# Gate maps of 32 of 48 quads of tokens built between the last 16 tiles of expert_u

## What is computed

```
act = gelu(einsum('td,tkd->tk', xt, expert_u[it]))
out = einsum('tk,tkd->td', gt * act, expert_v[it])
```

## Time and profile before

| | us |
|---|---|
| median of 3 runs | 1657.08 (1656.9 to 1657.41) |
| span of the profiled execution | 1656.2 |
| expert_u, tile 48 to the end of tile 62 (15 tiles) | 86.97 |
| gate stage, last tile of expert_u to the last map | 74.24 |
| expert_v, steady part | 286.44 |
| PE busy over the span | 1553.5 (94%) |
| DVE, ACT, POOL busy | 930.0, 688.0, 558.9 |

### The profile page before, as it was taken

One profiled execution on the slowest core, in us unless ns is written; L12 is line 12 of the kernel. 1 busy time (PEld: TensorE's weight loads), 2 busy tenths in 40 slices (PEclk: granted clock), 3 DMA queues, 4 the chain that ended last, 5 costly groups with the idle time before them and its releaser, 6 DMA issues.

```text
span 1656.2 us, 23309 instructions
## 1 busy us (share of the span) xinstructions
PE 1553.5 (94%) x9505; PEld 1219.7 (74%) x9505; DVE 930.0 (56%) x1472; ACT 688.0 (42%) x1017; POOL 558.9 (34%) x323
## 2 busy tenths in 40 slices
PE   7999999998898888999999999999998789999998
PEld 6788744443343434988899999999998668888886
DVE  5876422111111113686453887798434988988886
ACT  6565411101001003574453453444445975555554
POOL 3201100000000001322122434344555978787771
PEclk9999999999999999999999999999999999999999
DMA  8435999999999998535344555555566029999994
GB/s 295 145 120 194 422 399 421 421 421 421 421 421 421 421 421 342 197 128 191 102 157 152 190 192 187 173 201 184 197 232 215 1 96 337 348 347 349 357 340 161
DMA packets 99342, 444.80 MB, mean 269 GB/s; under 512 B 11152, under 2 KB 19856, under 8 KB 57632
## 3 DMA queue, kind: packets, MB, share of 16 engines
q1 hardware_dynamic: 86256, 404.90, 65.2%
q0 software_dynamic: 11264, 33.60, 5.5%
q10 hardware_dynamic: 1712, 4.76, 0.7%
HBM read 435.26 MB, written 7.86 MB: 268 GB/s over the span
## 4 chain that ended last, share of the span: by engine, by line
PE 66%; DMA 19%; DVE 7%; ACT 5%; issue 2%; POOL 0%; ACTq 0%; SPq 0%; DVEq 0%
DMA big<-in_w_up 11%; PE ps L483 11%; PE ps L485 11%; PE ps L484 11%; PE ps L1184 11%; PE ps L680 8%; PE ps L1176 7%; DMA fix<-in_w_up 3%; DMA hh<-in_w_up 3%; DVE fix_parts L1221 1%; PE ps L1152 1%; DMA fix<-in_w_in 1%; ACT fix_parts L2104 1%; ACT y L2522 1%; PE ps L663 1%
## 5 line engine op out<-in xcount | busy, mean ns | idle before, releaser
L2567 POOL TENSOR_TENSOR fix_parts<-fix,fix_parts 128x512 fp32r<-128x512 f32 x59 | 143.5, 2434 | 698.6 <-ACT fix_parts L2104 698.5
L485 PE MATMUL ps<-hh_parts,fix_parts 128*128 128x256 f32 x1120 | 317.3, 283 | 0.0
L680 PE MATMUL ps<-big 128*64 128x512 f32 x800 | 249.2, 595 | 17.8 <-DMA big<-in_w_up 9.2
L1221 DVE TENSOR_TENSOR fix_parts<-fix,fix_parts 128x1536 fp32r<-128x1536 f32 (+1 forms) x84 | 171.0, 2036 | 115.9 <-ACT fix_parts L2104 113.7
L483 PE MATMUL ps<-hh_parts,fix_parts 128*128 128x256 f32 x768 | 219.2, 285 | 6.8 <-issue 5.9
L484 PE MATMUL ps<-hl_parts,fix_parts 128*128 128x256 f32 x768 | 217.8, 284 | 0.0
L485 PEld LDWEIGHTS ps<-hh_parts,fix_parts 128*128 128x128 f32 x1120 | 215.2, 192 | 0.0
L680 PE MATMUL ps<-fix,big 128*64 128x512 f32 x528 | 189.4, 594 | 17.5 <-DMA big<-in_w_up 9.0
L2104 ACT ACTIVATE fix_parts<-fix 128x2048 fp32r<-128x2048 f32 x84 | 160.8, 1915 | 69.8 <-PE ps L1184 56.4
L680 PEld LDWEIGHTS ps<-big 128*64 128x64 f32 x800 | 79.7, 137 | 110.8 <-issue 110.0
L483 PEld LDWEIGHTS ps<-hh_parts,fix_parts 128*128 128x128 f32 x768 | 147.7, 192 | 8.2 <-issue 8.1
(11 more groups left out here) (416 smaller groups left out, 3664.4 us busy)
## 6 DMA issues: line engine op xcount, KB each, us to landing
fix<-in_expert_u SPq DMA_DIRECT2D x64, 1024.0 KB, 5.3
fix<-in_expert_v SPq DMA_DIRECT2D x38, 1024.0 KB, 7.6
big<-in_w_up SPq DMA_DIRECT2D x34, 1024.0 KB, 26.6
big<-in_w_down SPq DMA_DIRECT2D x34, 1024.0 KB, 25.6
big<-in_w_gate SPq DMA_DIRECT2D x32, 1024.0 KB, 26.1
big<-in_expert_v SPq DMA_DIRECT2D x26, 1024.0 KB, 7.5
fix<-in_w_gate SPq DMA_DIRECT2D x23, 1024.0 KB, 26.4
fix<-in_w_up SPq DMA_DIRECT2D x22, 1024.0 KB, 26.7
```

Source lines behind the costliest of these rows:

```text
L485: return pe.matmul(o, l[1], r[0], start=False, stop=last)
L680: ins = pe.matmul(m.PS[64 * i:64 * i + 64, bank, :], lhs(h * k_of // 2 + k, i), view(t.place[t.slot[x]])[:, k, c0:c0 + 512], start=(h + k ...
L1221: nc.vector.tensor_tensor(m.fr(x[:, 0:end]), x[:, 0:end], m.fr(hi[:, 0:end]).bitcast(F32), ALU.subtract).then_inc(s.lo_v, 1)
L2567: nc.gpsimd.tensor_tensor(m.fr(x[:, at:2048]), x[:, at:2048], m.fr(hi[:, at:2048]).bitcast(F32), ALU.subtract).then_inc(s.lo_g, 1)
```

## The change

`EARLY_AT = 48` and `EARLY = 32`. Behind the matmuls of each of the tiles 48 to 63 of expert_u, PE makes the maps of two quads, 32 in all (`early_quads`); the quads 32 to 47 follow after the last tile, as before.

- The one-hots of the early quads lie in three new places (two in `DS`, one in `Y`); the first wait for no tile. Each engine writes those of quads 2(i - 48) and 2(i - 48) + 1 in its iteration i: ACT after the high part of tile i + 1 and ahead of the gelus of tile i; DVE ahead of the low part of tile i + 1; POOL likewise.
- DVE weighs the two quads of iteration i - 1 in iteration i, in two instructions each: rows of `W` whose gelu is there are multiplied, the rows to come get a copy of the map.
- A tile from 48 on has its gelu of the tokens already mapped (8 to 128 of them) laid into `EA`, and DVE multiplies it into the maps in `W` (`weigh_acts`); ACT has three activations then, over the same 512 columns.
- DVE's `NG` (the negated gates) moves to the end of iteration 47. In the remaining quads DVE weighs two quads behind, not one.
- POOL fetches one sparse row at tile 48, since the places of the other two now hold one-hots; those two are fetched between the fourth and fifth pick, after the one-hots. The row sums begin in iteration 4 of expert_v instead of 3 (`sum_at`).

```diff
-    return 3 + a * 60 // SPARSE
+    return 4 + a * 59 // SPARSE
+def early_quads(i):
+    return range(2 * (i - EARLY_AT), 2 * (i - EARLY_AT) + 2) if EARLY_AT <= i < 64 else range(0)
+def early_from(q):
+    return EARLY_AT + q // 2
+def early_tokens(i):
+    return 8 * max(i - EARLY_AT + 1, 0)
...
+    rings = [DS[:, 2048:3072], DS[:, 3072:4096], part(512, 1024)], [EB[i // 2][:, 1024 * (i % 2):1024 * (i % 2) + 1024] for i in range(4)]
+    slot = lambda q: rings[0][q % 3] if q < EARLY else rings[1][q % 4]
+    m.EA = [DS[:, 256 * i:256 * i + 256] for i in range(2)]
...
+    def gate_map(q):
+        bank = q % 4
+        for sem in (s.e_a, s.e_v, s.e_g):
+            pe.wait_ge(sem, q + 1)
+        if q >= 4:
+            pe.wait_ge(s.weighed, q - 3)
+        for x in range(4):
+            ins = pe.matmul(m.PS[:, bank, x * P:(x + 1) * P], m.E1[q][:, x * P:(x + 1) * P],
+                            m.E2[q][:, x * P:(x + 1) * P], start=True, stop=True)
+        ins.then_inc(s.ghot, 1)
...
+        for q in early_quads(i):
+            gate_map(q)
+    for q in range(EARLY, DENSE // 4):
+        gate_map(q)
...
+def slot_open(eng, s, t, q):
+    if q < EARLY:
+        if q >= 3:
+            eng.wait_ge(s.ghot, q - 2)
+    elif q < EARLY + 4:
+        eng.wait_ge(s.used, t.used[t.first["expert_v"] - 1])
+    else:
+        eng.wait_ge(s.ghot, q - 3)
...
+    def weigh(q):
+        w, gates = m.W[:, :, 4 * q:4 * q + 4], m.PS[:, q % 4, :].rearrange("p (t n) -> p n t", t=4)
+        ve.wait_ge(s.ghot, q + 1)
+        if q >= EARLY:
+            ve.wait_ge(s.act, 64)
+            ve.tensor_tensor(w, gates, w, ALU.mult).then_inc(s.weighed, 1)
+            return
+        n = 2 * early_from(q)
+        ve.wait_ge(s.act, n // 2)
+        ve.tensor_tensor(w[:, 0:n, :], gates[:, 0:n, :], w[:, 0:n, :], ALU.mult)
+        ve.tensor_copy(w[:, n:P, :], gates[:, n:P, :]).then_inc(s.weighed, 1)
+    def weigh_acts(i):
+        tokens = early_tokens(i)
+        w = m.W[:, 2 * i:2 * i + 2, 0:tokens]
+        ve.wait_ge(s.act, i + 1)
+        ve.wait_ge(s.weighed, tokens // 4)
+        ve.tensor_tensor(w, m.EA[i % 2][:, 0:2 * tokens].rearrange("p (n t) -> p n t", n=2), w, ALU.mult).then_inc(s.early, 1)
+    for i in range(64):
+        for q in early_quads(i):
+            one_hots(q)
+        for q in early_quads(i - 1):
+            weigh(q)
+        dve_low(nc, m, s, t, first + i + 1)
+        if i > EARLY_AT:
+            weigh_acts(i - 1)
...
+    for q in range(EARLY, DENSE // 4):
+        one_hots(q)
+        weigh(q - 2)
+        if q - 2 == EARLY - 1:
+            weigh_acts(63)
...
+        tokens = early_tokens(i)
+        if tokens:
+            if i >= EARLY_AT + 2:
+                ac.wait_ge(s.early, i - EARLY_AT - 1)
+            ac.activation(m.EA[i % 2][:, 0:2 * tokens].rearrange("p (n t) -> p n t", n=2), src[:, :, SPARSE:SPARSE + tokens],
+                          ACT.Gelu_apprx_tanh)
+        ac.activation(m.W[:, 2 * i:2 * i + 2, tokens:DENSE], src[:, :, SPARSE + tokens:256], ACT.Gelu_apprx_tanh).then_inc(s.act, 1)
...
+    fetch(0)
+    for i in range(EARLY_AT, 64):
+        for q in early_quads(i):
+            one_hots(q)
+        if i < 63:
+            pool_low(nc, m, s, t, first + i + 1)
+    for q in range(EARLY, DENSE // 4):
+        one_hots(q)
...
+    po.wait_ge(s.ghot, EARLY)
+    for k in range(4):
+        pick(k)
+    for k in range(1, RING):
+        fetch(k)
+    for k in range(4, 8):
         pick(k)
```

More of the change, by code:

```diff
@@ L25 @@
 RING = 3
+EARLY_AT = 48
+EARLY = 32
 MOE_PLACES = (0, 1, 2, 3, 4, 5, 6, 9, 10, 11, 12, 13, 14, 15)
@@ L157, in signals @@
     s.ng, s.e_a, s.e_v, s.e_g = one("neg_gates"), one("one_hots_act"), one("one_hots_dve"), one("one_hots_pool")
-    s.ghot, s.weighed = one("gate_maps"), one("weighed")
+    s.ghot, s.weighed, s.early = one("gate_maps"), one("weighed"), one("acts_weighed")
     s.lists, s.moved, s.acts_kept = one("sparse_lists"), one("sparse_moved"), [one(f"acts_kept{i}") for i in range(2)]
@@ L1900, in vector_second, with one_hots @@
     first = t.split[f["expert_u"]]
[L1901 to L1905, removed]
-    I1T, I2T, GTT = m.keys
[L1908 to L1922, removed]
+    I1T, I2T, GTT = m.keys
+    def one_hots(q):
+        slot_open(ve, s, t, q)
         if q % 2:
             tt = 4 * q + 3
-            v.step(ve.tensor_scalar(m.E2[q % 4][:, 3 * P:4 * P], m.iota, I2T[:, tt:tt + 1], GTT[:, tt:tt + 1],
+            v.step(ve.tensor_scalar(m.E2[q][:, 3 * P:4 * P], m.iota, I2T[:, tt:tt + 1], GTT[:, tt:tt + 1],
                                     ALU.is_equal, ALU.mult))
-        ve.tensor_tensor(m.E1[q % 4].rearrange("p (t n) -> p t n", t=4),
+        ve.tensor_tensor(m.E1[q].rearrange("p (t n) -> p t n", t=4),
                          m.iota.rearrange("p (o n) -> p o n", o=1).broadcast_to((P, 4, P)),
@@ L2495, in scalar_second, with one_hots @@
     first = t.split[f["expert_u"]]
+    I1T, I2T, GTT = m.keys
+    def one_hots(q):
+        slot_open(ac, s, t, q)
+        if q >= 2:
+            ac.wait_ge(s.e_a, q - 1)
+        for x in range(2):
+            tt = 4 * q + x
+            o.step(ac.activation(m.SQS[q % 2][x], m.iota, ACT.Square, scale=-1.0, bias=I2T[:, tt:tt + 1]))
+        o.settle()
+        for x in range(2):
+            tt = 4 * q + x
+            ins = ac.activation(m.E2[q][:, x * P:(x + 1) * P], m.SQS[q % 2][x], ACT.Relu, scale=m.NG[:, tt:tt + 1],
+                                bias=GTT[:, tt:tt + 1])
+        ins.then_inc(s.e_a, 1)
     for i in range(64):
         act_high(nc, m, s, t, first + i + 1)
+        if i == EARLY_AT:
+            ac.wait_ge(s.ng, 1)
+        for q in early_quads(i):
+            one_hots(q)
         for what, b, _ in ROUTING.get(i, ()):
@@ L2584, in gpsimd_second @@
     po.wait_ge(s.joined, 1)
-    for n in range(t.n_first + 3, first + 53):
-        pool_low(nc, m, s, t, n)
+    I2T, GTT = m.keys[1:]
     table = a["expert_v_2"].rearrange("i p (j n) -> (i p j) n", j=4)
@@ L2592, in fetch, with one_hots @@
                               bass.IndirectOffsetOnAxis(m.vix[:, k:k + 1], 0)).then_inc(s.rows[k % RING], 16)
+    def one_hots(q):
+        slot_open(po, s, t, q)
+        for x in (2,) if q % 2 else (2, 3):
+            tt = 4 * q + x
+            ins = po.tensor_scalar(m.E2[q][:, x * P:(x + 1) * P], m.iota, I2T[:, tt:tt + 1], GTT[:, tt:tt + 1],
+                                   ALU.is_equal, ALU.mult)
+        ins.then_inc(s.e_g, 1)
+    for n in range(t.n_first + 3, first + EARLY_AT + 1):
+        pool_low(nc, m, s, t, n)
     po.wait_ge(s.r_keys, 2)
     po.wait_ge(s.moved, 32)
[L2596 to L2610, removed]
+    fetch(0)
+    for i in range(EARLY_AT, 64):
+        for q in early_quads(i):
+            one_hots(q)
+        if i < 63:
+            pool_low(nc, m, s, t, first + i + 1)
+    for q in range(EARLY, DENSE // 4):
+        one_hots(q)
     acts = actkeep.rearrange("p (n o) -> (p n) o", o=1)
```

33 lines of the change are left out of this document (10 added, 23 removed).

## The result

The changed kernel takes 1634.08 us (median of 4 runs, 1632.08 to 1634.83) against 1656.99 for the kernel before beside it: a ratio of 0.9865, 95% interval 0.9853 to 0.9876. By the medians that is 22.9 us less. The forecast was 19.0 less (1638.1). The span of the profiled execution is 1632.3 us, 23.9 less than before's 1656.2. That is 1.0 more than the medians say: in the runs of this study the time of a run is 1.6 to 1.7 us above its own span, so the traced execution of before took about 1657.8 us (an estimate), 0.8 above its median.

What follows compares the result with a forecast made beforehand. PE was taken to bound expert_u and expert_v, POOL and ACT together the gate stage. Terms: -48.4 + 29.6 + 0.3 - 0.5 = -19.0 us, giving 1638.1 us; range 1635.5 to 1645.5.

Steps and rivals of the forecast that it cites:

- the price of a pair of maps on PE: In expert_u, two maps behind a tile lengthen it by 1.97 us, bounded by 1.78 and 2.4; 15 pairs add 29.6 us.
- PE is the bound of expert_u and not of the gate stage: PE busy 86.63 of 86.97 us in expert_u; in the gate stage 52.34 of 74.24, POOL and ACT setting the pace.
- 32 quads less are 48.4 us less: Gate stage: with 32 of its 48 quads gone, it ends 48.36 us earlier.
- the 0.3 for DVE's extra work: After expert_u's last tile: DVE's two early weighs and a `weigh_acts` add 0.3 us, at most 1.5.
- 0.11 for a switch: Expert_u on PE: changing between tile matmuls and maps costs 0.11 us a pair, taken from three transposes after a tile.
- 0.08 for waits: Expert_u on PE: the eight waits at two maps add 0.08 us to each pair.
- The waits of PE are met a tile before: Expert_u: PE's new waits, for one-hots and the weighing of four quads earlier, are already met a tile before.
- The smallest cover: Tile 48, with POOL's row fetch: POOL's low part ends near 7 us after the gelu, against 7.5 for PE.
- POOL is the fullest, and it fits: Beside expert_u: POOL needs 5.2 to 6.8 us of a 7.73 us tile, ACT 5.5, DVE 5.7.
- 0.5 off for the fetches of rows: Expert_u: fetching one row instead of three at tile 52 takes away a wait felt by PE, saving 0.5 us.
- Rows come late in expert_v: Expert_v: DVE's waits for fetched rows could reach PE, costing 2 to 4 us, 1640 to 1642; chance 0.06.
- The exclusion lock: Expert_u: POOL and DVE can't work together, so a tile takes 9.2 us, 1662.7 in all; chance 0.05.

Runs made afterwards that it cites:

- half kernel: The changed kernel with 16 quads early, behind tiles 56 to 63, instead of 32: 1644.83 us, against 1634.57 for the changed kernel.
- late split: The changed kernel with the second map of each pair moved to the middle of the next tile: 1634.52 us, against 1634.57 for the changed kernel.

## What held in the prediction, and the step that failed

The mechanism held, and the time came out below the range. The step that failed is one term of the sum, the price of a pair of maps on PE: 1.97 us where it measured 1.78. The rest of the miss is smaller than what separates two executions.

- *PE is the bound of expert_u and not of the gate stage.* Right; it carried the direction and most of the size.
- *32 quads less are 48.4 us less.* Right to 0.6 in the first pair of traces and to 1.5 in the second: 47.45 and 46.6 went, where the forecast is 48.1 with the 0.3 for DVE's extra work. The half kernel gives the rate, 1.50 a quad. How much of the rest is DVE's work and how much variation was not looked into by a run.
- *A pair costs 1.97 us.* This is the step that failed. It is 1.78, tile after tile, in four traces: two of the changed kernel, the late split and the half. The bounds were right (1.78 and 2.4), and the value was taken inside them for two reasons that both proved empty: 0.11 for a switch, from the transposes, and 0.08 for waits. The transposes there are three instructions of another kind; their 0.44 us for 3 were no measure of a switch between products (what the 0.11 in them is, no run shows). 15 x 0.19 = 2.9 us of the 4.0 that the median lies below the forecast.
- *The waits of PE are met a tile before.* Right, PE was busy 118.87 of 118.87 us. The smallest cover was where the prediction put it, at the tile behind the fetch: POOL's low part ended 6.7 us after the gelu and PE took the tile at 7.3, for the foreseen 7 and 7.5. With the waits met, adding 0.08 a pair for them contradicted the prediction's own argument.
- *POOL is the fullest, and it fits.* Right: POOL 98.59, ACT 87.11, DVE 83.52 of 118.87, and POOL was still idle for 20 us of it. The cover held even at three quads a tile, except for the 0.39 us at tile 49.
- *0.5 off for the fetches of rows.* Right, 0.56.
- *Rows come late in expert_v.* The waits came (10.0 us of DVE) and never reached PE.
- *The exclusion lock turns it over.* Its mechanism is real, its point of decision far off: 7.54 us a tile against 8.85 where it became the bound. The rule by which the prediction weighed it, that weighs with a PSUM input fall out of the sum, gave 7.4 and thus no turn. The traces agree with the outcome, 7.54 us set by PE; no run tests that exemption by itself.
- *What was not in the sum*: 1.5 us of clock and 1.1 us of variation in untouched code, both of this one pair of traces. In the second pair the clock's 1.5 came again and of the 1.1 only 0.3; of the median's 4.0 us, 1.1 are left for all of it, and the medians can't divide them. The sum was made against a single execution that had the lower clock in a place where it costs; a window at the start of expert_v would have shown it (0.64), while the three stage windows of the earlier trace rows leave those 8 us out.
- *The range* ended below at 1635.5, nearly where the low bound of the pair alone leads (1635.2). The low price alone would have missed the range by 0.3 us, not by 1.4. The range left no room for what else could shorten the run, though the spread of the runs of before is by itself 2 us and more in this study (1652.63 to 1657.65 in 13 runs). That is the lesson on its width: the bounds of a term and the variation of an execution add up.

## What to carry to other kernels

Where one engine is the bound in a stage and idles in the next, moving its work costs its dense price (the distance of the starts in a full stream, here 0.111 us a record), and what comes back is the pace of the stage that it leaves (1.50 us a quad): compare those two numbers first, and go on moving until the engine that prepares the work becomes the bound. Here all 48 quads could be moved, three a tile (ratio 0.9825), before that came; it came when POOL alone made six one-hots a tile. Add nothing for a switch or for waits on a supposition; test for it by splitting the block and counting the distance between tiles, but only at a place where its inputs are ready. And before a clock effect is put down to a stage, look for the lower level in every trace at hand, not only in the one where it was noticed.

## What the runs showed of the hardware

- Float32 products of 128x128x128 inside a stream of rounded 128x256 ones take 0.222 us each (two records of 0.111), with no price for the change: tiles 7.54 us apart with two maps together, 7.53 to 7.54 with the maps apart.
- Where POOL's and DVE's low parts met, the one that began later stood until the other was done, or nearly so: POOL's ended 1.15 us after DVE's end, and DVE's took 2.42 us for 1.76. Six one-hots and a low part, 5.8 us of work, took 8.85 us a tile on POOL beside DVE.
- The granted clock fell to the lower level for some 3 us behind a PE hole of 1.65 us in one trace and stayed up behind one of 2.5 us in another; where it fell at the start of expert_v, the first tile took 8.06 to 8.22 us for 6.54 to 6.70.
